# Two softmaxes with the maximum negated as it is taken, q scaled at its drain, and one output half written by ScalarE

## The reference, cut to what matters

```
# sliding window: 8 heads of 64, 2 key groups, window 128, a sink per head
m = maximum(max(s), sink);  p = exp(s - m);  p = p / (sum(p) + exp(sink - m))

# cross attention: 4 heads of 256, plain softmax

# sparse attention: 16 heads of 64, 4 key groups, causal here (256 tokens, all blocks chosen)
q = rope(x @ w_q)
o = g0 * softmax(q kc / 8) vc + g1 * softmax(q ks / 8) vs + g2 * softmax(q kw / 8) vw
```

## Time and profile before

| | |
|---|---|
| median of 3 runs | 2443.29 us |
| lowest and highest run | 2440.86, 2446.21 us |
| span of the profiled execution | 2441.5 us |
| the profiled execution's own time | not shown apart from its span |
| granted TensorE clock, mean | 0.989 |
| sliding window's softmax | about 91 to 115 us of the span |
| sparse attention's softmax | about 1309 to 1374 us of the span |

### The profile page before, as it was taken

How to read it: one execution, slowest core, us unless ns; L and a number is a source line. 1 busy time by engine, 2 the same in 40 slices (tenths; PEclk the granted TensorE clock), 3 DMA queues, 4 the chain that set the end, 5 groups by cost and what they waited for, 6 DMA issues and landing times.

```text
span 2441.5 us, 37168 instructions
## 1 busy us (share of the span) xinstructions
PE 2357.2 (97%) x15482; PEld 2137.1 (88%) x15482; DVE 1876.2 (77%) x2060; ACT 1342.6 (55%) x1306; POOL 2.4 (0%) x8
## 2 busy tenths in 40 slices
PE   6899999999999999999999899999999999999997
PEld 6799999999999999899997778888888888888886
DVE  5666696878665978654557668889888989898987
ACT  4546333454444334433434447776777777777775
POOL 0000000000000000000000000000000000000000
PEclk9999999999999999999999999999999999999999
DMA  5233355532343455455432239999999999999995
GB/s 217 86 121 138 124 187 179 193 139 104 130 140 137 161 185 179 155 180 185 161 107 76 70 135 374 375 359 344 359 376 358 343 360 375 359 343 360 374 360 216
DMA packets 163270, 556.85 MB, mean 228 GB/s; under 512 B 8608, under 2 KB 8736, under 8 KB 124832
## 3 DMA queue, kind: packets, MB, share of 16 engines
q1 hardware_dynamic: 161904, 547.45, 61.5%
q10 hardware_dynamic: 1008, 6.49, 0.7%
q0 software_dynamic: 192, 0.52, 0.1%
HBM read 552.86 MB, written 1.05 MB: 227 GB/s over the span
## 4 chain that ended last, share of the span: by engine, by line
PE 70%; DVE 3%; ACT 3%; issue 1%; DMA 1%; DVEq 0%; ACTq 0%; SPq 0%
PE ps L1563 12%; PE ps L1565 12%; PE ps L1564 12%; PE ps L968 9%; PE ps L970 8%; PE ps L969 8%; PE ps L1079 2%; PE ps L1048 1%; ACT whi L548 1%; PE ps L1542 1%; DMA raw<-stream 1%; PE ps L1331 1%; PE ps L1609 0%; DVE x L2502 0%; DVE small L1838 0%
## 5 line engine op out<-in xcount | busy, mean ns | idle before, releaser
L1722 DVE TENSOR_TENSOR wlo<-raw,whi 128x2048 fp32r<-128x2048 f32 x519 | 1186.2, 2290 | 277.8 <-ACT whi L548 218.8
L548 ACT ACTIVATE whi<-raw 128x2048 fp32r<-128x2048 f32 x519 | 994.0, 1916 | 592.1 <-PE ps L970 366.6
L968 PE MATMUL ps<-hh,whi 128*128 128x256 f32 x2080 | 597.3, 287 | 9.6 <-DVE hl L1790 7.0
L969 PE MATMUL ps<-hl,whi 128*128 128x256 f32 x2080 | 592.0, 285 | 0.0
L970 PE MATMUL ps<-hh,wlo 128*128 128x256 f32 x2080 | 592.0, 285 | 0.0
L968 PEld LDWEIGHTS ps<-hh,whi 128*128 128x128 f32 x2080 | 402.6, 194 | 12.4 <-DVE hl L1790 7.4
L969 PEld LDWEIGHTS ps<-hl,whi 128*128 128x128 f32 x2080 | 402.7, 194 | 0.3
L970 PEld LDWEIGHTS ps<-hh,wlo 128*128 128x128 f32 x2080 | 402.3, 193 | 0.0
L1563 PE MATMUL ps<-whi,hh 128*128 128x512 f32 x896 | 359.3, 401 | 2.0 <-DVE hl L2453 2.0
L1565 PE MATMUL ps<-wlo,hh 128*128 128x512 f32 x896 | 351.8, 393 | 0.0
L1564 PE MATMUL ps<-whi,hl 128*128 128x512 f32 x896 | 350.4, 391 | 0.0
(11 more groups left out here) (341 smaller groups left out, 2695.3 us busy)
## 6 DMA issues: line engine op xcount, KB each, us to landing
raw<-stream SPq DMA_DIRECT2D x519, 1024.0 KB, 5.4
work<-w_in ACTq DMA_DIRECT2D x1, 2240.0 KB, 10.1
stage<-stage_consts ACTq DMA_DIRECT2D x4, 512.0 KB, 4.8
work<-mem_in ACTq DMA_DIRECT2D x2, 1024.0 KB, 5.4
x<-x_in SPq DMA_DIRECT2D x1, 1024.0 KB, 4.9
out<-x SPq DMA_DIRECT2D x4, 256.0 KB, 2.3
const<-consts SPq DMA_DIRECT2D x1, 548.5 KB, 5.8
work<-work POOLq DMA_DIRECT2D x4, 128.0 KB, 2.9
```

What stands on the lines that cost most here:

```text
L548: nc.scalar.activation(whi[hi_at(g, odd)][:, :], raw[g % RAWS][:, :], ACT.Copy).then_inc(hi_ready, 1)
L968: mm(out_ap, hi_w, hi_x, start=start, stop=False, **kw)
L969: mm(out_ap, hi_w, lo_x, start=False, stop=False, **kw)
L1722: V.tensor_tensor(wlo[g % RAWS][:, :], raw[g % RAWS][:, :], whi[hi_at(g, odd)][:, :].bitcast(F32), ALU.subtract).then_inc(lo_ready[g % RAW ...
```

## The change

The reduction writes the negated maximum. In the sparse attention nothing follows it: it releases the exponentials itself, whose scale is now 1.0, because q is multiplied by 1/8 when it is drained. In the sliding window the combination with the sink takes the minimum with a negated sink, the second small operation adds the sink and releases ScalarE; the product with -1 is gone. The negated sinks are made once, ahead of that stage. In cross attention the product with the negative scale becomes one with the positive. In the sparse attention the high half of an output is written by ScalarE (`out_hi`), at the start of the step in which TensorE computes the values of the second branch and ahead of that step's exponentials; VectorE waits for it before it writes the low half. ScalarE's loop has one step more.

```diff
--- before.py
+++ after.py
@@ -291,6 +291,7 @@
         cmp_turned = sem("cmp_turned")
         cmp_ready = sem("cmp_ready")
         nsa_roped = sem("nsa_roped")
+        nsa_out_hi = sem("nsa_out_hi")
         keys_swapped = sem("keys_swapped")
 
         logits_t = sem("logits_t")
@@ -607,9 +608,17 @@
                     nc.scalar.activation(small[:, s0 + 12:s0 + 16], small[:, s0 + 8:s0 + 12], ACT.Exp)
                 for h in range(4):
                     ins = nc.scalar.activation(probs[:, h * 256:h * 256 + nk], scores[:, h * 256:h * 256 + nk],
-                                               ACT.Exp, scale=score_scale(kind), bias=small[:, s0 + h:s0 + h + 1],
+                                               ACT.Exp, scale=1.0 if kind == "nsa" else score_scale(kind), bias=small[:, s0 + h:s0 + h + 1],
                                                accum_out=small[:, s0 + 4 + h:s0 + 5 + h])
                 ins.then_inc(exp_done, 1)
+
+            def out_hi(u, unit):
+
+                g, qt, _ = unit
+                o = NSA_O + (u - NSA_U) // 2
+                act.wait_ge(pv_done, u + 1)
+                view = hh[:, :].rearrange("p (b c) -> p b c", b=NB)[:, 2 * g:2 * g + 2, qt * P:(qt + 1) * P]
+                nc.scalar.activation(view, r3(banks(o_bank("nsa", o))[:, 0:2 * P], 2), ACT.Copy).then_inc(nsa_out_hi, 1)
 
             def softmax_act(kind, u0, between=None):
                 if kind != "nsa":
@@ -617,10 +626,12 @@
                 if between is not None:
                     between[-1]()
                 us = units(kind)
-                for step in range(len(us) + 2):
+                for step in range(len(us) + 3 * (kind == "nsa") + 2 * (kind != "nsa")):
+                    if kind == "nsa" and step >= 3 and us[step - 3][2]:
+                        out_hi(u0 + step - 3, us[step - 3])
                     if step < len(us):
                         exponentials(kind, u0 + step, P * key_tiles(kind, us[step][1]), SCORE_BANK[(u0 + step) % 2])
-                    if step >= 2:
+                    if 2 <= step < len(us) + 2:
                         u = u0 + step - 2
                         nk = P * key_tiles(kind, us[step - 2][1])
                         act.wait_ge(pt_ready, u + 1)
@@ -1835,25 +1846,31 @@
             def maxima(kind, u, g, nk, bank):
                 s0 = STATS[u % 3]
                 dve.wait_ge(scores_ready, u + 1)
-                link(V.tensor_reduce(small[:, s0:s0 + 4], r3(banks(bank), 4)[:, :, 0:nk], AX, ALU.max))
+                largest = V.tensor_reduce(small[:, s0:s0 + 4], r3(banks(bank), 4)[:, :, 0:nk], AX, ALU.max, negate=True)
+                if kind == "nsa":
+                    largest.then_inc(negmax_ready, 1)
+                    return
+                link(largest)
                 if kind == "swa":
                     link(V.scalar_tensor_tensor(out=small[:, s0:s0 + 4], in0=small[:, s0:s0 + 4], scalar=score_scale(kind),
-                                                in1=R("sinks", 4 * g, 4), op0=ALU.mult, op1=ALU.max))
-                    link(V.tensor_tensor(small[:, s0 + 8:s0 + 12], R("sinks", 4 * g, 4), small[:, s0:s0 + 4], ALU.subtract))
-                V.tensor_scalar(small[:, s0:s0 + 4], small[:, s0:s0 + 4], -1.0 if kind == "swa" else -score_scale(kind), None,
-                                ALU.mult).then_inc(negmax_ready, 1)
+                                                in1=small[:, 632 + 4 * g:636 + 4 * g], op0=ALU.mult, op1=ALU.min))
+                    V.tensor_tensor(small[:, s0 + 8:s0 + 12], small[:, s0:s0 + 4], R("sinks", 4 * g, 4), ALU.add).then_inc(negmax_ready, 1)
+                else:
+                    V.tensor_scalar(small[:, s0:s0 + 4], small[:, s0:s0 + 4], score_scale(kind), None, ALU.mult).then_inc(negmax_ready, 1)
 
             def normalise(kind, u, g, qt, br):
                 pr, s0, nk = PROBS[u % 3], STATS[u % 3], P * key_tiles(kind, qt)
                 dve.wait_ge(exp_done, u + 1)
                 if kind == "swa":
                     link(V.tensor_tensor(small[:, s0 + 4:s0 + 8], small[:, s0 + 4:s0 + 8], small[:, s0 + 12:s0 + 16], ALU.add))
-                link(V.reciprocal(small[:, s0 + 16:s0 + 20], small[:, s0 + 4:s0 + 8]))
                 if kind == "nsa":
                     at = 64 + qt * 48 + g * 12
-                    coef = small[:, s0 + 16:s0 + 20].rearrange("p (par j) -> p par j", par=2)
-                    link(V.tensor_tensor(coef, coef, small[:, at:at + 12].rearrange(
-                        "p (j par b) -> p par j b", j=2, par=2)[:, :, :, br + 1], ALU.mult))
+                    two = lambda a: small[:, a:a + 4].rearrange("p (par j) -> p par j", par=2)
+                    link(V.reciprocal(small[:, s0 + 16:s0 + 20], small[:, s0 + 4:s0 + 8]))
+                    link(V.tensor_tensor(two(s0 + 16), small[:, at:at + 12].rearrange(
+                        "p (j par b) -> p par j b", j=2, par=2)[:, :, :, br + 1], two(s0 + 16), ALU.mult))
+                else:
+                    link(V.reciprocal(small[:, s0 + 16:s0 + 20], small[:, s0 + 4:s0 + 8]))
                 for h in range(4):
                     ins = V.tensor_scalar(pr[:, h * 256:h * 256 + nk], pr[:, h * 256:h * 256 + nk],
                                           small[:, s0 + 16 + h:s0 + 17 + h], None, ALU.mult)
@@ -1876,14 +1893,17 @@
                         if br == branches - 1:
                             o = o0 + (st - 3) // branches
                             dve.wait_ge(pv_done, u + 1)
-                            evacuate(o, o_blocks(g), qt * P, o_bank(kind, o))
-
-            def evacuate(o, blocks, col, bank, width=P):
+                            evacuate(o, o_blocks(g), qt * P, o_bank(kind, o), split=kind == "nsa")
+
+            def evacuate(o, blocks, col, bank, width=P, split=False):
 
                 b0, n = blocks
                 view = lambda t: t[:, :].rearrange("p (b c) -> p b c", b=NB)[:, b0:b0 + n, col:col + width]
                 src = banks(bank)[:, 0:n * width].rearrange("p (b c) -> p b c", b=n)
-                link(V.tensor_copy(view(hh), src))
+                if split:
+                    dve.wait_ge(nsa_out_hi, o - NSA_O + 1)
+                else:
+                    link(V.tensor_copy(view(hh), src))
                 V.tensor_tensor(view(hl), src, view(hh).bitcast(F32), ALU.subtract).then_inc(o_drained, 1)
 
             def conv_ffn(layer, l, alpha):
@@ -2079,6 +2099,7 @@
 
             proj_copy("ab_in", 0, {1: lambda: round_mask(1), 2: swa_squares, 4: swa_normed, 6: swa_rope, 8: swa_keys_copied})
             step(V.tensor_scalar(W(6, 4), W(6, 4), 64 ** -0.5, None, ALU.mult))
+            step(V.tensor_scalar(small[:, 632:640], R("sinks", 0, 8), -1.0, None, ALU.mult))
             dve.wait_ge(v_turned, 1)
             step(V.tensor_copy(W(37), ps[:, 4, 0:256]))
             V.tensor_copy(W(38, 4), banks(5)).then_inc(v_copied, 1)
@@ -2343,7 +2364,7 @@
                     qt, odd = n // 2, n % 2
                     step(V.scalar_tensor_tensor(out=rows[:, 8 * n:8 * n + 8, :],
                                                 in0=ps[:, 6 + odd, qt * 120:(qt + 1) * 120].rearrange("p (a n) -> p a n", n=NCMP),
-                                                scalar=64 ** -0.5, in1=C("cmp_mask", qt * 15, 15).unsqueeze(1).to_broadcast([P, 8, NCMP]),
+                                                scalar=1.0, in1=C("cmp_mask", qt * 15, 15).unsqueeze(1).to_broadcast([P, 8, NCMP]),
                                                 op0=ALU.mult, op1=ALU.add))
                 sync()
                 link(V.tensor_reduce(small[:, 512:544], rows, AX, ALU.max))
@@ -2364,7 +2385,8 @@
             ph = PHASES["nsa_in"]
             for p in range(ph.n):
                 split_lo(ph.g + p + AHEAD)
-                drain(ph, p, lambda bank, s: V.tensor_copy(W(2 * NSA_SLOTS[s], 2), ps[:, bank, :]))
+                drain(ph, p, lambda bank, s: V.tensor_scalar(W(2 * NSA_SLOTS[s], 2), ps[:, bank, :],
+                                                             64 ** -0.5 if NSA_SLOTS[s] < 4 else 1.0, None, ALU.mult))
                 if p == 0:
                     round_mask(4)
                 if p == 1:
```

## The result

The changed kernel takes 2458.22 us (median of 4 runs, 2456.83 to 2459.68) against 2443.56 for the one before: +14.7 us, a ratio of 1.0059 with an interval of 1.0047 to 1.0071. The forecast was +4.9 (2448.2), its range ended at 2453.0. The profiled execution took 2459.10 us, its span is 2457.2.

A forecast was written before the change was run, and what follows sets the result against it. A chain of waits was taken to bound the sparse attention, its cost passed on through a full TensorE. Loop +5.0, tail +0.1 and sliding window -0.17 gave +4.9 us, 2448.2 from the median 2443.29; range 2442.5 to 2453.0.

The forecast's parts named there:

- The loop: Sparse attention: even units' exponentials wait for earlier values and the copy; 16.23 us for four units against 14.71, +5.0; chance 0.50.
- the second rival: Sparse attention: the loop holds but without the slow stretch from 1320 to 1325 us; +3.7, 2447.0; chance 0.20.
- Negation: Maxima of sparse attention and sliding window: each link 0.20 us shorter, -0.4 for two links, -0.17 in the window.
- The drain: Projection ahead of the sparse attention: scaling q at its ten copies out of PSUM, 692 ns each, adds 0.
- the cost of the copy: ScalarE's high half in the sparse attention: 393 ns each, the exponential behind it starts 0.30 us later.
- The first rival: Sparse attention: maxima stay the bound, waits for values hide behind them; -2.0 with the window, 2441.3; chance 0.10.
- the third rival: Sparse attention: TensorE's idle time brings more slow stretches, 1.7 us for each of three groups; +4.9 + 5.1, 2453.3; chance 0.15.
- The sign that I had named for being wrong: Sparse attention: 14.3 us for four units, a clock below 1.00 past 1325 us, or drains above 0.69.
- TensorE's mean load: Sparse attention: about 13.4 us of 16.2 per four units, more than 2.82 of 5; held against more slow stretches.

## Why the prediction was wrong

The direction was right, the size was a third of what came, and 2458.22 lies outside the range.

**The loop** was right, in its mechanism and its numbers: 8.79 and 7.44 were forecast, 8.76 and 7.37 measured. Both stages at the full clock, the change costs +3.9 us; the sum without the slow stretch (the second rival) was +3.7, of which -0.17 lies in the sliding window, so +3.9 too. Unit 4's exponentials start 14.27 us after the first maximum, before 12.73: +1.54, against +1.6 forecast.

**Negation** was right: 0.20 us a link (14.3 against 14.7 for four units with the high half on VectorE), 0.2 in the sliding window, nothing in the reduction. **The drain** at 691 ns was right, and so was the cost of the copy: 0.38, the next instruction 0.28 later. The first rival, the gain kept, was excluded by the order of the two queues, as argued; it comes true when the high half goes back to VectorE (2441.86, where that rival gave 2441.3). The Trainium skill's rule on saturated engines ("Perfetto Trace Analysis", section "Optimizing Scalar/DVE Operations") would have the move to ScalarE pay where VectorE is saturated. VectorE was at 69%, and the swap, worth about nothing by that rule, costs 16 us against the version without it (2458.22 and 2441.86): what decided was the place in the queue, and there the measurement stands.

**The step that failed is the third rival, more slow stretches:** its price and its chance. I gave it 0.15 and one stretch of 1.7 us for each of three groups, +5.1. The clock took 80.29 - 66.64 = 13.7 us in the stage, and the matmuls behind it about 2 more, as they began in a low stretch. A group costs more than 1.7: units 8 to 12 took 20.76 us in place of 16.12, 4.6 more, for one low stretch of six microseconds (near 1340 to 1346) and a second one in the round behind it. The sign that I had named for being wrong, a clock below 1.00 past 1325 us, came at 1340.

The chance rested on TensorE's mean load, 13.4 us of 16.2, which lay above the 2.82 of 5 ahead of the fall in the kernel before. That comparison did not hold. The 13.4 were a little high, as they had a slow stretch in them: the pauses of 1.81 and 1.38 in 16.13 leave 12.9. And the load is uneven. Just ahead of the fall TensorE has 3.19 us of work in five (1335 to 1340 above). The emptiest five in the loop of the kernel before have more:

```profile
1347.60:1352.60 5.00, 3.65 (x39) 2.82 (x38) 4.08 (x13) 3.42 (x13) 0.00 (x0) 1.00 0.00 0
```

But that decides nothing by itself: the window from 1322 to 1327 has the same 3.19 in the same profile and no fall behind it, and the kernel before gets through 2.57 at the end of its stage (1362 to 1367) at 1.00. What decides it stays open. What the runs show is that the falls go with the pauses, since they are gone when these are filled.

The whole adds up so: 2458.22 - 2443.92 = 14.3 us come back when the new kernel's pauses are filled, and 3.5 in the kernel before, where the clock takes time too. The difference of the two, 10.8, and the 3.8 of the loop make the 14.7 to within 0.1.

A second error lies under it: I read the one slow stretch of a single profiled execution as all that the kernel has. The stretch near unit 4 does recur: eight of the nine profiles in which the pause at step 3 is not filled have it. But its length differs, and others come and go: two profiles of the kernel before have 63.37 and 68.67 us where 62.75 is the full clock's, the second with a slow stretch at the end of the stage that the first lacks, the first with 3 us more in the projection ahead. A forecast made at both levels of the clock would have been about +3.9 where it holds, and where it falls up to half of the slowed time on top; how much would be slowed no row of before shows.

What the Trainium skill says in the section "Matmul Optimizations" of the same page, that the matmul engine scales its power with its utilization and matmuls should therefore come back to back, spoke for this rival. No run shows the power, but the granted clock agrees: with the same work, the same order and the same waits, the stage takes 80.3 us at 0.79 with the pauses and 66.6 at 1.00 with zeros in them. I had weighed it and given it too little.

## What to carry to other kernels

An instruction moved to a less busy engine brings its wait with it, and everything behind it in that queue waits too. Behind the work that others wait for it does less harm, but then look at what still waits for it on the engine that it left; or leave it where its own queue has the time. When a change lengthens TensorE's pauses, price the loop twice, at both levels of the clock, compare the pauses one by one and not only the mean load, and don't take one profile's slow stretches for the kernel's. And fill the pauses with zeros in a copy of both kernels before comparing them: it takes the clock's chance out of that stage (not out of the rest, the runs of the filled versions still lie 5 to 12 us apart), and here it paid by itself.

## What the runs showed that I had not expected

- The kernel before is 3.5 us faster with 32 matmuls of zeros in three pauses of one stage (ratio 0.9983), and with the negated maxima and the high half on VectorE 6.1 us (0.9973).
- Filling one pause of 2 us (step 3) did not do away with low stretches: in that profile one came 40 us later, at the next place where TensorE had little to do.
- With the wait alone ahead of six exponentials the median is 2449.1 us, with the copy behind it, 0.3 us more on ScalarE each time, 2458.2. Of the runs with the wait alone, half had hardly any loss. What decides it from run to run stays open.
